# Rows of maxima and decay weights of an mLSTM chunk: spread to 128 partitions by DRAM and not by eight products on TensorE

## The reference

```python
b = jnp.cumsum(lf, axis=-1)
d_log = jnp.where(causal, b[..., :, None] - b[..., None, :] + ig[..., None, :], -jnp.inf)
inter = b + m[..., None]
m_t = jnp.maximum(inter, jnp.max(d_log, axis=-1))
s = jnp.einsum('bhtd,bhsd->bhts', q, k) * jnp.exp(d_log - m_t[..., None])
w_inter = jnp.exp(inter - m_t)
num = w_inter[..., None] * jnp.einsum('bhvd,bhtd->bhtv', C, q) + jnp.einsum('bhts,bhsv->bhtv', s, v)
...
C_new = decay[..., None, None] * C + jnp.einsum('bhs,bhsv,bhsd->bhvd', w_state, v, k)
```

## Time and profile before

| | us |
|---|---|
| median of 3 runs | 2550.44 (2547.42 to 2551.92) |
| the profiled execution, its time | 2544.0 |
| its span | 2542.4 |
| of it the 15 steps 0 to 14 | 621.7 |
| PE busy, whole span | 2286.9 (90%) |
| DVE busy | 1472.2 (58%) |
| ACT busy | 971.6 (38%) |
| POOL busy | 460.6 (18%) |

### The profile page before, as it was taken

One profiled execution on the slowest core, in us unless ns is written; L12 is line 12 of the kernel. 1 busy time (PEld: TensorE's weight loads), 2 busy tenths in 40 slices (PEclk: granted clock), 3 DMA queues, 4 the chain that ended last, 5 costly groups with the idle time before them and its releaser, 6 DMA issues. The chain is left out here.

```text
span 2542.4 us, 34289 instructions
## 1 busy us (share of the span) xinstructions
PE 2286.9 (90%) x10843; PEld 1856.3 (73%) x10844; DVE 1472.2 (58%) x2806; ACT 971.6 (38%) x1567; POOL 460.6 (18%) x619
## 2 busy tenths in 40 slices
PE   6998988889839999999668999999999999969998
PEld 5787777777737888888556777777777777747776
DVE  4566666756553554555545446666666568645554
ACT  3333232333232222222144445555555557623332
POOL 0002124412002232223211000000000000013332
PEclk9888898998869999999779999999999999989999
DMA  6010111111052232223079566778777759744431
GB/s 205 29 59 37 69 54 58 54 58 54 26 192 84 91 116 99 103 91 115 20 281 346 184 255 227 285 291 310 261 284 289 280 185 386 280 164 141 140 140 63
DMA packets 156822, 407.05 MB, mean 160 GB/s; under 512 B 16363, under 2 KB 19875, under 8 KB 156510
## 3 DMA queue, kind: packets, MB, share of 16 engines
q1 hardware_dynamic: 135014, 337.15, 36.9%
q0 software_dynamic: 14560, 43.11, 5.0%
q10 hardware_dynamic: 7200, 26.22, 2.5%
HBM read 330.10 MB, written 84.82 MB: 163 GB/s over the span
## 5 line engine op out<-in xcount | busy, mean ns | idle before, releaser
L1922 DVE TENSOR_TENSOR w_lo<-raw,w_hi 128x2048 fp32r<-128x2048 f32 x196 | 436.1, 2287 | 71.9 <-ACT w_hi L1858 71.7
L1858 ACT ACTIVATE w_hi<-raw 128x2048 fp32r<-128x2048 f32 x196 | 359.8, 1927 | 69.2 <-DMA raw<-in_w 66.9
L199 PE MATMUL bank<-w_hi,mix_x_hi 128*128 128x512 f32 x680 | 291.6, 429 | 54.8 <-DMA mix_x_lo<-xT_dram 39.1
L1823 PE MATMUL bank<-w_hi,x_hi 128*128 128x512 f32 x784 | 310.9, 397 | 2.1 <-DVE x_lo L1914 2.1
L1824 PE MATMUL bank<-w_lo,x_hi 128*128 128x512 f32 x784 | 310.8, 396 | 0.0
L1825 PE MATMUL bank<-w_hi,x_lo 128*128 128x512 f32 x784 | 310.7, 396 | 0.0
L200 PE MATMUL bank<-w_lo,mix_x_hi 128*128 128x512 f32 x680 | 282.3, 415 | 0.0
L201 PE MATMUL bank<-w_hi,mix_x_lo 128*128 128x512 f32 x680 | 282.0, 415 | 0.0
L199 PEld LDWEIGHTS bank<-w_hi,mix_x_hi 128*128 128x128 f32 x680 | 140.2, 206 | 85.9 <-DMA mix_x_lo<-xT_dram 34.1
L1823 PEld LDWEIGHTS bank<-w_hi,x_hi 128*128 128x128 f32 x784 | 147.8, 189 | 38.2 <-issue 2.5
L1825 PEld LDWEIGHTS bank<-w_hi,x_lo 128*128 128x128 f32 x784 | 147.7, 188 | 35.8
(11 more groups left out here) (296 smaller groups left out, 4388.4 us busy)
## 6 DMA issues: line engine op xcount, KB each, us to landing
raw<-in_w SPq DMA_DIRECT2D x96, 2048.0 KB, 11.5
y_dram<-y_sb ACTq DMA_DIRECT2D x50, 512.0 KB
raw_all<-in_w_in SPq DMA_DIRECT2D x24, 512.0 KB, 6.0
xT_dram<-mix_x_hi SPq DMA_DIRECT2D x17, 512.0 KB, 2.7
xT_dram<-mix_x_lo SPq DMA_DIRECT2D x17, 512.0 KB, 3.6
mix_x_hi<-xT_dram SPq DMA_DIRECT2D x17, 512.0 KB, 3.7
mix_x_lo<-xT_dram SPq DMA_DIRECT2D x17, 512.0 KB, 4.5
x_sb<-in_x_prompt SPq DMA_DIRECT2D x16, 512.0 KB
```

The lines of the kernel that those rows point to most:

```text
L199: pe.matmul(bank[:, :], x_hi[:, k, :], wh[:, k, :], start=(k == 0), stop=False)
L1823: pe.matmul(bank[:, :], x_hi[:, k, :], wh[:, k, :], start=(k == 0), stop=False)
L1858: return act.activation(out, in_, ACT.Copy)
L1922: dve.tensor_tensor(w_lo[slot(j, m)][:, cols], raw[m][:, cols], w_hi[slot(j, m)][:, cols].bitcast(F32), ALU.subtract).then_inc(lo_ready, 1)
```

## The change: what it does

The eight products and `sel4` go. Once `em_ready` is raised for a chunk, SP writes rows 4 and 6 to a DRAM tensor of 2 x 512 numbers, waits for both to land, and reads each back as a broadcast to 128 partitions, row 4 into `dm` and row 6 into `qs`. DVE works on them in place. For chunk t + 1 this is in SP's step t, behind `keep_ha(t - 1)`; for chunk 0 it stands ahead of `load_samples`. Since `dm` and `qs` are now written by a DMA while the chunk before may still be read, ACT's `row_exps(t)` waits for `kw_ready` and `num_mm` of the chunk before. PE's step now begins with a wait for `em_ready`, and the wait for `hh_ready` moves to `numerators`.

```diff
+                            def spread_rows(t):
+
+                                sp_.wait_ge(em_ready, t + 1)
+                                for w in range(2):
+                                    sp_.dma_start(rows_dram[w].rearrange("(h n) -> h n", h=H), rows[:, 4 + 2 * w, :]).then_inc(rows_kept, 16)
+                                sp_.wait_ge(rows_kept, 32 * t + 32)
+                                for w, dst in enumerate((dm, qs)):
+                                    sp_.dma_start(dst[:, :, :].rearrange("p h n -> p (h n)"), rows_dram[w].partition_broadcast(P)).then_inc(rows_spread, 16)
...
                                 if not isinstance(t, int) or t > 0:
                                     keep_ha(t - 1)
+                                if at(t, NT - 1):
+                                    spread_rows(t + 1)
...
+                            spread_rows(0)
                             load_samples()
...
-                            def spread_rows(t):
-                                pe.wait_ge(rows_ready, t + 1)
-                                if not isinstance(t, int) or t > 0:
-                                    pe.wait_ge(hh_ready, t)
-                                for h in range(H):
-                                    ins = pe.matmul(heads(N[0])[:, h, :], sel4[:, h, :], rows[:, 4, :], start=True, stop=True)
-                                ins.then_inc(mb_mm, 1)
-                                pe.wait_ge(em_ready, t + 1)
-                                for h in range(H):
-                                    ins = pe.matmul(heads(N[1])[:, h, :], sel4[:, h, :], rows[:, 6, :], start=True, stop=True)
-                                ins.then_inc(wib_mm, 1)
+                            def row_columns(t):
                                 pe.transpose(COLS[:, 0:H], rows[:, 0, :], ident[0:H, 0:H])
...
                             def numerators(t):
-                                pe.wait_ge(dlog_ready, t + 1)
                                 pe.wait_ge(qs_ready, t + 1)
+                                if not isinstance(t, int) or t > 0:
+                                    pe.wait_ge(hh_ready, t)
...
                             def step(t):
                                 more = at(t, NT - 1)
+                                pe.wait_ge(em_ready, t + 1)
                                 if more:
                                     x_transposes(t + 2)
-                                spread_rows(t)
+                                row_columns(t)
...
                             def row_exps(t):
+                                if not isinstance(t, int) or t > 0:
+                                    act.wait_ge(kw_ready, t)
+                                    act.wait_ge(num_mm, t)
                                 act.wait_ge(rows_ready, t + 1)
...
-                                dve.wait_ge(mb_mm, t + 1)
+                                dve.wait_ge(rows_spread, 32 * t + 32)
                                 for h in range(H):
-                                    ins = TS(dm[:, h, :], heads(N[0])[:, h, :], cols[:, h:h + 1], 0.0, ALU.add, ALU.min)
+                                    ins = TS(dm[:, h, :], dm[:, h, :], cols[:, h:h + 1], 0.0, ALU.add, ALU.min)
...
-                                dve.wait_ge(wib_mm, t + 1)
-                                if not isinstance(t, int) or t > 0:
-                                    dve.wait_ge(num_mm, t)
-                                st.do(dve.tensor_copy(decay[:, :], heads(N[1])[:, :, P - 1]))
-                                TT(qs[:, :, :], qkT[:, 0:H, :], heads(N[1]), ALU.mult).then_inc(qs_ready, 1)
+                                st.do(dve.tensor_copy(decay[:, :], qs[:, :, P - 1]))
+                                st.settle()
+                                TT(qs[:, :, :], qkT[:, 0:H, :], qs[:, :, :], ALU.mult).then_inc(qs_ready, 1)
```

More of the change, by code:

```diff
@@ L99, in program @@
         sm_dram = dram("sm_dram", (TB, VQ))
+        rows_dram = dram("rows_dram", (2, H * P))
         PS = [whole.enter_context(nc.psum_tensor(f"bank{i}", [P, 512], F32)) for i in range(8)]
@@ L248, in program @@
                     gate_b = s1("gate_b", [H, 2])
-                    sel4 = s1("sel4", [H, H, P])
                     tri_c = s1("tri_c", [P, P])
@@ L280, in program @@
                      o_mm, gates_mm, gates_in, gates_tp, qtok_in, qk_tp, qk_in, conv_ready, qk_tanh, qkT_ready, gate_abs, gate_ln,
-                     rows_ready, em_ready, pw_steps, v_in, o_in, sg_ready, mb_mm, wib_mm, cols_mm, s_mm, k_tp, dlog_ready, dm_exp,
+                     rows_ready, em_ready, pw_steps, v_in, o_in, sg_ready, rows_kept, rows_spread, cols_mm, s_mm, k_tp, dlog_ready, dm_exp,
                      dm_ready, qs_ready, sp_ready, kw_ready, num_mm, st_mm, state_done, hh_ready, hh_sq, hh_rstd, ha_ready,
@@ L285, in program @@
                          "o_mm gates_mm gates_in gates_tp qtok_in qk_tp qk_in conv_ready qk_tanh qkT_ready gate_abs gate_ln "
-                         "rows_ready em_ready pw_steps v_in o_in sg_ready mb_mm wib_mm cols_mm s_mm k_tp dlog_ready dm_exp "
+                         "rows_ready em_ready pw_steps v_in o_in sg_ready rows_kept rows_spread cols_mm s_mm k_tp dlog_ready dm_exp "
                          "dm_ready qs_ready sp_ready kw_ready num_mm st_mm state_done hh_ready hh_sq hh_rstd ha_ready "
@@ L1019, in _ @@
                             pool.memset(neghalf[:, :], -0.5).then_inc(p_steps, 1)
-                            pool.memset(sel4[:, :, :], 1.0).then_inc(p_steps, 1)
                             pool.iota(iota_i[:, :], pattern=[[-1, NE]], base=NE, channel_multiplier=0).then_inc(p_steps, 1)
                             pool.iota(tok[:, :], pattern=[[0, 1]], base=0, channel_multiplier=1).then_inc(p_steps, 1)
-                            pool.wait_ge(p_steps, 7)
+                            pool.wait_ge(p_steps, 6)
                             pool.affine_select(out=ident[:, :], in_=ident[:, :], compare_op=ALU.not_equal, fill=1.0, base=0,
@@ L1034, in _ @@
                                                pattern=[[1, P]], channel_multiplier=-1).then_inc(p_steps, 1)
-                            pool.affine_select(out=sel4[:, :, :], in_=sel4[:, :, :], compare_op=ALU.is_equal, fill=0.0, base=0,
-                                               pattern=[[1, H], [0, P]], channel_multiplier=-1).then_inc(p_steps, 1)
                             pool.tensor_copy(rank32[:, :], iota_i[:, :]).then_inc(p_steps, 1)
@@ L1039, in _ @@
                             pool.tensor_scalar(rank4[:, :], iota_i[:, NE - NG:], 1.0, None, ALU.mult).then_inc(p_steps, 1)
-                            hold(pool, p_steps, 13)
+                            hold(pool, p_steps, 11)
                             pool.sem_inc(const_done, 1)
```

## The result

| | before | after |
|---|---|---|
| median, us | 2549.99 (5 runs, 2545.4 to 2551.9) | 2561.95 (5 runs, 2556.5 to 2564.6) |
| the profiled execution, its time | 2544.0 | 2564.6 |
| its span | 2542.4 | 2563.0 |
| of it steps 0 to 14 | 621.7 | 638.3 |

The ratio is 1.0051, with a 95% interval of 1.0037 to 1.0065: slower by 12.0 us by the medians, 13.0 by the ratio, or by 9 to 17. Forecast were 2570.6 and +20.2.

What follows compares the result with a forecast made beforehand. The prediction took steps 0 to 14 to be bound by PE and what PE waits for. Terms -1.9 + 11.0 + 5.7 + 5.4 = +20.2 us, added to the median 2550.4, gave 2570.6 us, range 2554 to 2588.

Steps and rivals of the forecast that it cites:

- The products hid a wait: PE, steps 0 to 14: the products fill the q projection's wait for DVE's low half; removing them gains nothing.
- The first rival: PE before the q projection: products are on the path after all; -6.1 us, 2544.3; chance 0.08.
- Step 15, -1.9: Last step, nothing to transpose or project: columns for DVE's chain come 1.9 us sooner, so -1.9 us.
- SP ahead of step 0, +11.0: SP's queue: waiting for em_ready of chunk 0 sends load_x(3) late, delaying ACT, DVE and PE; +11.0 us, bounds 8 and 14.
- the second rival: SP's queue ahead of step 0 is no loss, its long issuing compressible: +9.2 us, 2559.6; chance 0.11.
- The hooks, +5.7: SP's hooks behind the spreading: load_c late, POOL delays steps 9 (+3.3) and 10 (+2.4); +5.7 us, between 2 and 9.
- The way through memory, 0: Every step: writes and broadcasts through DRAM end 6.6 us before DVE wants them, so cost 0.
- The fourth rival: Rows come too late in each step, the chain taking 18 us: +55, about 2626; chance 0.05.
- The granted clock, +5.4: PE's new idle time lowers its clock: 0.5 us a step in 11 steps, +5.4 us, bounds 0 and 12.
- the bound of 0: Lower bound of the clock's cost on PE: 0 if products filling only 4 of 128 rows already counted as idle.
- The third rival: PE's clock costs its full price in every step: 12 us instead of 5.4, 2577.2; chance 0.12.
- keep their form: DVE's four additions, now reading SBUF, keep their form; only the product with two SBUF operands slows, hidden, cost 0.

Runs made afterwards that it cites:

- e4: e3 with the eight products, `sel4` and the old wait for `hh_ready` put back, results read by nobody, rows still by memory: 2546.86 us, ratio 0.9997.
- e8: Kernel before with eight more products of row 4 ahead of the eight already there, results overwritten: 2584.49 us, ratio 1.0149.
- e3: Kernel after with SP's queue reordered at both places: samples' loads ahead of chunk 0's rows, hooks ahead of the spreading of rows: 2542.21 us, ratio 0.9983.
- e7_trips3: e3 with three more awaited writes of row 4 ahead of the broadcasts: 2542.23 us, ratio 0.9981.
- e5: e3 with the four score products of chunk t moved ahead of the q projection, into PE's wait: 2522.68 us, 0.9904; repeated, 2516.38 us, 0.9877.
- e7_trips6: e3 with six more awaited writes of row 4 ahead of the broadcasts: 2545.27 us, ratio 0.9998.
- e6: Kernel before, eight products in place, with the four score products moved from behind the q projection to ahead of it: 2540.96 us, ratio 0.9974.
- e2: Kernel after with only SP's hooks for the samples moved ahead of the spreading of rows, step 0 left as it is: 2555.01 us, ratio 1.0031.

## Why the prediction was right, and where it was not

**The products hid a wait: shown.** The q projection starts when it did, PE waits 1.8 to 1.9 us in twelve steps, and longer in steps 3, 4 and 12 (2.35, 4.95 and 3.08, before 2.09, 3.12 and 1.25). e4 puts the products back at 0.9 us in steps 0 to 14, and e8 shows that the q projection's start is on the path once they outlast the wait. The first rival, 20.9 us to gain, is gone; its weak point was that it asked how long PE was busy and not what PE would do next.

**Step 15, -1.9: as measured.** From the step's beginning to the transposes of k, PE took 7.71 us before and takes 5.71 now:

```profile
730.87 1.11 PE L568 MATMUL bank<-ident,qkT 128*128 128x128 f32 x4 [4.34 <-DVE sp L918]
```

with the step's beginning at 725.16 (before, 715.89 less 708.18).

**SP ahead of step 0, +11.0: 10.4 and 12.8 by the runs, 8.9 by the step's window.** `load_x(3)` went out at 102.63, forecast near 104, ACT's squares came 15.5 us later than before (16.2), and the convolution at 111.13 (112.6). What shortened it: from em_ready (79.23) to the first small load (81.71) it took 2.5 us, not 3.1, and the issuing of the 33 transfers 20.5 (81.71 to 102.17), against 22.1 before. So the second rival, which needed half of that, falls, and with it the idea that x and xT in flight had made the issuing long, but for 1.6 us.

**The hooks, +5.7: 5.1 and 6.9 by the runs, 7.6 and 5.8 by windows.** POOL waited for quarter 2 for 3.2 us; forecast, 3.3. Its waits in all:

```profile
POOL raw_all L1063 <- DMA raw_all<-in_state_C: 6.5, 2, 3.3
```

Both waits are of that size. I had taken off 0.93 us of idle time from the second; whether that was right, 5.7, or the two waits count in full, 6.6, the four measures do not tell. The loads of quarters took 5.7 us to land in the median, not 4.6 and perhaps 0.6.

```profile
dm<-rows_dram SPq DMA_DIRECT2D x15, 256.0 KB, 3.1
qs<-rows_dram SPq DMA_DIRECT2D x15, 256.0 KB, 3.7
...
raw_all<-in_state_C SPq DMA_DIRECT2D x4, 512.0 KB, 5.7
```

**The way through memory, 0: right.** em_ready to landing is 464.76 to 466.70 + 3.7 = 470.4, that is 5.6 us and not 7.7; DVE uses the columns at 476.95. The fourth rival supposed that a row read 128 times might be slow; it takes 3.1 to 3.7 us for 256 KB. The new chain never came close to deciding a step.

**The granted clock, +5.4: this is the step that failed.** I had divided the difference of steps 4 and 8, 0.8 us beyond the wait, by the wait, as though the products that PE does in a step's first 2 us were work to the throttle and the wait that replaced them were not. In e3 and e4, equal but for the products, the stretch is 621.45 and 622.39 us at 0.88 and 0.89, and the q projection has slow products in 13 of 15 steps of both. Over the stretch they have 236 and 226 slow products; ten of them, 2 us, is all that could be called a price, it does not show in the sum, and e7_trips3, which has e3's PE stream, has 257. The medians have e3 4.7 us under e4, where the term wanted it 3.5 above. So the runs bear out the bound of 0, "if products that fill only 4 of 128 rows counted as idle already", which I named and chose against: thin products did no better than an empty gap, while four full products in the same place brought the start of step 6's q projection from 0.57 to 1.00 (e5). The Trainium skill (TensorE: Matmul & The Clock Gate, What's actually happening) says that the throttle is the default and activity lifts it; e5 agrees with that. The third rival falls with the term. There is a slip in the working besides: the kernel before has a wait at this place in five steps (3, 4, 9, 10 and 12), so ten steps and not 11 had none, and the term would have been +4.9, the first rival's gain 19.0 and not 20.9.

The forecast without that term is +14.8. Measured are +12.0 with an interval of 9 to 17. The likeliest sum was too high by its last term, and the lower bound of the range was set low enough, since it took the clock at nothing.

**What is left open.** e3 should have been 1.9 us faster than before and is 5.3 (2 to 7 by its interval), and after should be e3 + 19.7 and is e3 + 17.3. The first is at the edge of its interval, the second within it, and nothing in the traces was found for them. Nor does the number of slow products alone give a step's length: e7_trips6 has 59 more of them than e3 in a stretch that is 2.8 us shorter (618.65). The profiled execution is 20.6 us longer than before's, of which 16.6 less 2.0 lie in the steps: the other 6 lie in stages that the change doesn't touch, almost all behind step 15, and were not followed up; the medians differ by 12.0 only.

## What to carry to other kernels

An operation that takes time on the bounding engine is worth what its successor can use: look at when the successor's other inputs are ready before counting. A transfer that is itself free can cost in the queue that issues it, if it brings a wait: count what stands behind the wait, and put it where nothing with an earlier use is behind. And room that is won is worth something only with work that can fill it: here the change costs 12 us as it stands, gives 2 to 7 with its queue mended, and 24 to 32 with four full products moved into the gap. Of these some 7 can be had by the same move in the kernel before, without the change (e6).

## What the runs showed of the hardware

**What fills a gap on PE matters, and not only how long it is.** The clock fell to its lower level 3 to 5 us behind a step's beginning in 13 of 15 steps with nothing in the gap (e3) and in 13 with eight products of 4 rows (e4). With four products of 128 rows straight behind the transposes it did so in one (e5), and not in the step where 1.99 us of gap were left. With the same four behind the eight thin ones, and the q projection close on them, it fell in eleven (e6), as in the kernel before. So it matters what PE does there and also when; which of the two differences between e5 and e6, the thin products or the later place of the full ones, decides was not tried. Where it fell, the q projection had some eight slow products, 1.6 us. They are 103 of the 236 slow products in e3 and 101 of the 260 in the kernel before; the others stand further on in the steps.

**DVE's form with SBUF operands is quicker alone and far slower beside POOL.** The four additions read `dm` in SBUF now. I had said that they "keep their form"; their speed is not kept. All of their instances, the kernel before and then after (shortest, median, longest in ns):

```profile
L888 DVE TENSOR_SCALAR dm<-bank,cols x64: 340/343/352, 89.8 to 711.3; 128x128 f32<-128x128 f32 x64
```

```profile
L895 DVE TENSOR_SCALAR dm<-dm,cols x64: 273/281/2427, 90.0 to 726.3; 128x128 f32<-128x128 f32 x64
L901 DVE TENSOR_TENSOR qs<-qkT,qs x16: 691/692/2932, 91.0 to 726.7; 128x512 f32<-128x512 f32 x16
```

From PSUM the additions took 340 to 352 ns in every case, beside POOL or not; from SBUF 281 in the median and up to 2427. In step 9, where POOL works at a quarter of the samples at that time:

```profile
477.25 2.99 DVE L895 TENSOR_SCALAR dm<-dm,cols 128x128 f32<-128x128 f32 x4
480.34 2.93 DVE L901 TENSOR_TENSOR qs<-qkT,qs 128x512 f32<-128x512 f32 x1
```

I had expected it of the product with two SBUF inputs alone, and it reaches a TENSOR_SCALAR with its input and its output in SBUF, too. The Trainium skill (SBUF — State Buffer, Who interferes with whom) names `tensor_scalar` among the instructions that can take the ports shared with GpSimd, and these rows agree. The forecast held it hidden, since DVE waits for POOL's masked `dm` right behind. In e2 step 10 takes 40.89 us (before 40.86) and step 9 takes 40.90 (39.11). The 1.8 us in step 9 need not be this: there the q projection starts 0.2 us later than before and has 7 slow products where before it had none, 1.4 us. A step's length moves by as much from one kernel to the next elsewhere (step 3, 43.39 before and 40.79 after).

**An awaited small write is short.** The next issue came 1.5 us after the start of two awaited writes of 2 KB, and 1.16 us after that of a lone one; a store of 256 KB, from which I had taken it, lands 2.0 us after its issue.
